# Two stages with rounded operand pairs, four column sums beside stick-breaking, and the first expert rows picked by one-hot products

## What is computed

```python
# first block
mod = silu(c) @ ada_w + ada_b                 # six rows of 1024: shift1, scale1, gate1, shift2, scale2, gate2
y_a = nsa_attention(...) @ w_up_nsa           # 512x512 @ 512x1024
y_b = stick_breaking_attention(...) @ w_up_sb # 512x512 @ 512x1024
mixed = (sigmoid(m_a) * y_a + sigmoid(m_b) * y_b) @ w_out   # 512x1024 @ 1024x1024
h = h + gate1 * mixed
u2 = rms_norm(h, norm2_g) * (1 + scale2) + shift2
h = h + gate2 * (square(relu(u2 @ mlp_w1)) @ mlp_w2)
# second block, its last part: top-1 group of 4, top-2 experts of 8 in it, 32 experts in all
ffn = hierarchical_moe(hn2, ...)   # each expert: (silu(x @ w_gate[e]) * (x @ w_up[e])) @ w_down[e]
x = rms_norm(x + gate2 * ffn, g_final)
```

## Time and profile before

| | |
|---|---|
| median of 3 runs | 1868.61 us (1866.4 to 1873.15) |
| profiled execution, its time | 1867.54 us |
| its span | 1865.8 us |
| PE busy | 1677.0 us, 90% |
| DVE busy | 748.5 us, 40% |
| ACT busy | 482.7 us, 26% |
| POOL busy | 195.3 us, 10% |
| mean granted clock | 0.956 of full |

### The profile page before, as it was taken

The page is one execution under the profiler, slowest core; times in us unless marked ns, Lnnn a source line. Parts: engine busy times, 40 slices in busy tenths (PEclk is TensorE's granted clock), DMA queues, the critical chain, the costliest instruction groups (busy, mean ns, idle before and its releaser), DMA issues. The chain is left out here.

```text
span 1865.8 us, 20533 instructions
## 1 busy us (share of the span) xinstructions
PE 1677.0 (90%) x7854; PEld 1113.4 (60%) x7855; DVE 748.5 (40%) x1298; ACT 482.7 (26%) x799; POOL 195.3 (10%) x260
## 2 busy tenths in 40 slices
PE   5999998988899999999998999889499999998772
PEld 4788887756444778878886778767333333332220
DVE  6344215744565777522225555353411111111113
ACT  4322324545001322222224532252211111110001
POOL 1020000000112122200003000001111111110101
PEclk9999999978999999999999999999699999999996
DMA  9424220020654467522221222105999997999995
GB/s 301 107 68 135 83 76 1 1 91 0 248 183 159 173 238 261 172 77 92 103 98 35 68 91 68 68 1 200 421 402 418 420 380 299 419 418 420 419 420 218
DMA packets 114466, 366.26 MB, mean 196 GB/s; under 512 B 21695, under 2 KB 24939, under 8 KB 89779
## 3 DMA queue, kind: packets, MB, share of 16 engines
q1 hardware_dynamic: 105055, 347.06, 49.4%
q0 software_dynamic: 5760, 9.02, 1.4%
q10 hardware_dynamic: 3540, 8.69, 1.3%
HBM read 359.85 MB, written 16.84 MB: 202 GB/s over the span
## 5 line engine op out<-in xcount | busy, mean ns | idle before, releaser
L2221 PE MATMUL x_upa<-x_ring,x_Ta 128*64 128x512 f32 x608 | 136.8, 599 | 16.4 <-DMA x_ring<-in_w_expert_up_dram 16.4
L2221 PE MATMUL x_gpa<-x_ring,x_Ta 128*64 128x512 f32 x608 | 138.7, 606 | 12.9 <-DMA x_ring<-in_w_expert_gate_dram 10.7
L2221 PEld LDWEIGHTS x_upa<-x_ring,x_Ta 128*64 128x64 f32 x608 | 45.5, 138 | 105.2 <-issue 105.2
L2221 PEld LDWEIGHTS x_gpa<-x_ring,x_Ta 128*64 128x64 f32 x608 | 45.8, 140 | 103.0 <-issue 103.0
L325 DVE TENSOR_TENSOR p_lo<-p_raw,p_hi 128x2048 fp32r<-128x2048 f32 (+1 forms) x20 | 44.8, 2238 | 139.1 <-ACT p_hi L625 139.1
L332 PE MATMUL fr_p<-p_hi,u_high 128*128 128x512 f32 x224 | 89.8, 401 | 0.0
L333 PE MATMUL fr_p<-p_lo,u_high 128*128 128x512 f32 x224 | 88.7, 396 | 0.0
L334 PE MATMUL fr_p<-p_hi,u_low 128*128 128x512 f32 x224 | 88.4, 395 | 0.0
L2246 PE MATMUL x_y0a<-x_ring,x_aTa 128*64 128x512 f32 x304 | 72.9, 600 | 5.6 <-ACT x_aTa L2288 4.5
L2283 ACT ACTIVATE x_siga<-x_gpa 128x512 f32<-128x512 f32 x19 | 11.3, 597 | 253.7 <-PE x_gpa L2221 253.7
L2246 PE MATMUL x_y1a<-x_ring,x_aTa 128*64 128x512 f32 x304 | 71.8, 592 | 0.0
(11 more groups left out here) (770 smaller groups left out, 3822.0 us busy)
## 6 DMA issues: line engine op xcount, KB each, us to landing
x_ring<-in_w_expert_gate_dram SPq DMA_DIRECT2D x64, 1024.0 KB, 23.3
x_ring<-in_w_expert_up_dram SPq DMA_DIRECT2D x64, 1024.0 KB, 27.6
x_ring<-in_w_expert_down_dram SPq DMA_DIRECT2D x64, 1024.0 KB, 25.8
p_raw<-in_w_in_dram SPq DMA_DIRECT2D x18, 1024.0 KB, 5.2
adaw0m<-in_w_ada_dram SPq DMA_DIRECT2D x6, 2048.0 KB, 10.2
adaw1m<-in_w_ada_dram SPq DMA_DIRECT2D x6, 2048.0 KB, 9.5
w_raw0m<-in_mlp_w_dram SPq DMA_DIRECT2D x8, 1024.0 KB, 7.1
w_raw1m<-in_mlp_w_dram SPq DMA_DIRECT2D x8, 1024.0 KB
```

What stands on the lines that cost most here:

```text
L2221: mm = nc.tensor.matmul(ps[CAP * f:CAP * f + CAP, :], self.xT[:, k, CAP * f:CAP * f + CAP], w[m + f][k // 4][:, k % 4, :], start=(k == 0), ...
```

## The change

Four things change.

1. The mixing and the output projection use `matmul3` on rounded pairs. The splitting is done by ACT copies and DVE `low` operations in the same blocks. The separate turning block of the first branch is gone: its flip products stand at the head of `mix_branches`. The turning of the mixture writes high and low parts (`turn_split`).
2. The column sums of modulation units 0 to 3 are made by a new class `FirstSums`, one operation at a time, between DVE's steps of stick-breaking. Unit 4 is summed in the mixing, units 5 to 7 in the output projection.
3. The rows of the first round are no longer gathered. DVE makes a one-hot matrix `picks` (128 places for each tile of tokens), and PE multiplies the normalised rows, which are still in memory, with it: 32 float32 products of 128x128, which come out already turned.
4. The gate products of round 1 move into `norm_route`, ahead of the block's end. The clearing of `x_ga` moves from `norm_route` to the head of `first_places`. In SP's list the load of slot 9, where the normalised rows lie, now comes after the parked slot and also waits for the picking products.

```diff
@@ class FirstSums (new)
+    def load(self, sp):
+        for u, (m, n) in enumerate(self.units):
+            for half in range(2):
+                ks = slice(4 * half, 4 * half + 4)
+                if u:
+                    sp.wait_ge(self.added, KD * (u - 1) + 4 * half + 4)
+                sp.dma_start(self.wbuf[:, ks, :], eights(self.w, m * D + 512 * n, 512)[:, ks, :]).then_inc(self.landed[half], 16)
+    def add(self, dve, count):
+        v = self.nc.vector
+        for j in range(self.done, min(self.done + count, KD * len(self.units))):
+            u, k = j // KD, j % KD
+            a, x, c = self.acc[u], self.wbuf[:, k, :], self.sc[:, k:k + 1]
+            if k % 4 == 0:
+                dve.wait_ge(self.landed[k // 4], 16 * u + 16)
+            if k == 0:
+                v.tensor_scalar(a[:, :], x, c, None, ALU.mult).then_inc(self.added, 1)
+            else:
+                dve.wait_ge(self.added, j)
+                v.scalar_tensor_tensor(out=a[:, :], in0=x, scalar=c, in1=a[:, :], op0=ALU.mult, op1=ALU.add).then_inc(self.added, 1)
@@ stick_breaking, DVE
+                    sums_of.add(dve, 4 if n % 2 else 1 if n else 0)
                     if n >= 3 and n % 2:
                         take((n - 3) // 2)
                     plus(n)
+                    sums_of.add(dve, 1 - n % 2)
                     lows(n)
+                    sums_of.add(dve, 2 * (1 - n % 2))
+                sums_of.add(dve, 1)
                 take(heads // 2 - 1)
@@ mix_branches, PE
+                    if b == 0:
+                        pe.wait_ge(heads_low, 4)
+                        pe.wait_ge(w_low, 1 if n == 0 else 3)
+                    elif n:
+                        pe.wait_ge(w_low, 2)
+                    for k in range(4):
+                        if i == 0 and b == 1:
+                            pe.wait_ge(second_low, 2 * k + 2)
+                        mm = matmul3(nc, ps[i % 2][b][:, :], (high[b][0][:, k, P * t:P * t + P], low_of[b][0][:, k, P * t:P * t + P]),
+                                     (high[b][1 + n][:, k, :], low_of[b][1][:, k, cols(n)]), k == 0, k == 3)
...
+                products(0, 1)
+                products(1, 1)
+                close(0)
+                close(1)
@@ mix_branches, ACT (new)
+                act.wait_ge(w_in[1], 16)
+                for k in range(4):
+                    copy(high[1][1][:, k, :], wu[1][:, k, cols(0)], second_high)
+                    copy(high[1][0][:, k, :], B.oT[1][:, k, :], second_high)
+                for k in range(4):
+                    act.wait_ge(turned, k + 1)
+                    copy(high[0][0][:, k, :], tps[k][:, :], heads_high)
+                act.wait_ge(w_in[0], 16)
+                for b, n in rest:
+                    copy(high[b][1 + n][:, :, :], wu[b][:, :, cols(n)], w_high)
@@ ResidualOut.dve
+        low(v, self.low[0][:, 4:8, :], self.first_w[:, 4:8, :], self.high[1][:, :, 0:512]).then_inc(self.first_low, 1)
+        mod.sum(dve, u)
+        for j in range(2):
+            dve.wait_ge(self.w_high, j + 1)
+            low(v, self.low[1][:, 4 * j:4 * j + 4, :], self.raw[:, 4 * j:4 * j + 4, :],
+                self.high[j][:, :, 512:1024]).then_inc(self.w_low, 1)
+        mod.sum(dve, u + 1)
@@ norm_route, SP
-                sp.wait_ge(stored, 16)
-                ring.load(sp, 9)
                 sp.wait_ge(parked, 16)
                 ring.load(sp, PARKED)
+                sp.wait_ge(stored, 16)
+                sp.wait_ge(first_turned, 4)
+                ring.load(sp, 9)
@@ norm_route, POOL
-                X.begin(pool)
-                pool.wait_ge(X.cleared, 1)
+                X.begin(pool, clear=False)
+                pool.sem_inc(X.ids_ready, 1)
                 pool.wait_ge(stored, 16)
-                pool.wait_ge(tokens, 1)
-                X.gather(pool, 1, 0)
@@ norm_route, PE
+                pe.wait_ge(picked, 1)
+                for k in range(KD):
+                    for t in range(NT):
+                        mm = nc.tensor.matmul(first_ps[k // 2][:, P * (k % 2):P * (k % 2) + P], xn[:, t, cols(k)], picks[:, t, :],
+                                              start=(t == 0), stop=(t == NT - 1))
+                    if k % 2:
+                        mm.then_inc(first_turned, 1)
+                pe.sem_inc(X.turned, 2)
+                table_of(0)
+                w, arrived = ring.of(0), ring.arrived(0)
+                X.half_hidden(pe, 1, w, arrived, 0, 0)
+                table_of(1)
+                X.half_hidden(pe, 1, w, arrived, 0, 1)
@@ residual_up, SP
-                sp.wait_ge(mod1.summed, len(mod1.units))
+                sp.wait_ge(mod1.summed, len(mod1.units) - mod1.first)
                 sp.wait_ge(mod1.spread_out, len(mod1.units))
@@ first_places
+                pool.memset(X.xg[:, :], 0.0).then_inc(X.cleared, 1)
                 X.scatter_nothing(pool)
```

More of the change, by code:

```diff
@@ L141, with __init__ @@
 class Modulation:
-    def __init__(self, s, nc, C, M, cols, w, bias, parts, tag, gain=None):
+    def __init__(self, s, nc, C, M, cols, w, bias, parts, tag, gain=None, summed=0, acc=None):
+        self.first = summed
         self.eights, self.eights_from = {}, []
@@ L1436, in _ @@
             def _(sp):
-                ahead(sp)
+                ahead(sp, sums_of)
             @block.tensor
@@ L1637, in _, with products @@
             def _(sp):
-                for u in range(2, 6):
-                    mod.load_unit(sp, u)
-                    if u == 2:
-                        ahead(sp)
+                load_units(sp)
+                sp.wait_ge(ready, NT)
+                load_first(sp)
+                mod.load_unit(sp, 6)
             @block.tensor
             def _(pe):
-                for i, (t, n) in enumerate(parts):
+                def products(i, b):
+                    t, n = parts[i]
                     if i >= 2:
@@ new lines, in _ @@
+                for k in range(4):
+                    for t in range(NT):
+                        mm = nc.tensor.matmul(tps[k][:, P * t:P * t + P], B.oa[:, t, P * k:P * k + P], C.flip[:, :],
+                                              start=True, stop=True)
+                    mm.then_inc(turned, 1)
+                products(0, 1)
+                products(1, 1)
+                close(0)
+                close(1)
+                for i in range(2, len(parts)):
+                    products(i, 1)
+                    close(i)
@@ L1712, in pe @@
                 for k in range(KD):
[L1713 to L1714 removed]
+                    if b == 0 and k == 4:
+                        pe.wait_ge(self.first_low, 1)
+                    mm = matmul3(self.nc, self.banks[b % 6][:, :], [a[:, k, P * t:P * t + P] for a in self.aT],
+                                 (self.high[k // 4][:, k % 4, 512 * n:512 * n + 512], self.low[n][:, k, :]), k == 0, k == KD - 1)
                 mm.then_inc(self.ready, 1)
@@ L1887, in _, with table_of @@
                 mm.then_inc(counts, 1)
-                for m in range(2):
+                def table_of(m):
                     for h in range(2):
@@ L1917, in _ @@
                 nc.scalar.activation(R.w[:, :, 1:2], d[:, :, :], ACT.Exp).then_inc(exp2, 1)
+                for k in range(4, KD):
+                    act.wait_ge(first_turned, k // 2 + 1)
+                    nc.scalar.activation(X.xT[:, k, :], first_ps[k // 2][:, P * (k % 2):P * (k % 2) + P], ACT.Identity,
+                                         scale=scale[:, k:k + 1], bias=shift[:, k:k + 1]).then_inc(X.modulated[1], 1)
             @block.vector
@@ L2206, in turn, with half_hidden @@
         mm.then_inc(self.turned, 1)
-    def hidden(self, pe, i, w, arrived):
+    def half_hidden(self, pe, i, w, arrived, m, half):
         nc = self.nc
-        for m, ps, ready in ((0, self.gps, self.gate_ready), (2, self.ups, self.up_ready)):
+        ps, ready = (self.ups, self.up_ready) if m else (self.gps, self.gate_ready)
+        if half == 0:
             if m == 0:
@@ L2386, in _, with multiply @@
                 ran = count(pe, "multiply")
-                for b in range(2):
-                    X.turn(pe, 1, b)
-                def multiply(i, w, arrived):
-                    X.hidden(pe, i, w, arrived)
+                def multiply(i, w, arrived, begun=False):
+                    X.hidden(pe, i, w, arrived, begun)
                     X.turn(pe, i + 1, 0)
@@ L3081, in _ @@
                 O.dve(dve)
-                for i in range(NT, NT + 2):
-                    O.take(dve, i)
+                O.take(dve, NT + 1)
                 W.low(dve, 0)
@@ L3340, in program, with load_up @@
                     wu = [beside.sb(f"wu{i}", [P, 4, D]) for i in range(2)]
-                    def load_up(sp):
+                    parts, accs = [2, 4, 3, 5], [M[1].gate[j][:, 512 * n:512 * n + 512] for j in range(2) for n in range(2)]
+                    first_sums = lambda s: FirstSums(s, nc, M[0].sc, A["ada_w"][0], [(m, n) for m in parts[:2] for n in range(2)], accs)
```

(2 more changed lines are left out.)

299 lines of the change are left out of this document (197 added, 102 removed).

## The result

The changed kernel takes 1864.46 us in the median of 20 runs (1854.01 to 1872.3), the kernel before 1871.55 us beside it (1863.28 to 1893.64). The ratio is 0.995, with a 95% interval of 0.9933 to 0.9966: by the ratio 9.4 us less (6.4 to 12.5; the two medians stand 7.1 apart), where 15.7 were forecast. The profiled execution took 1868.54 us, with a span of 1866.7 us at a mean granted clock of 0.950, which is the second slowest of its 20 runs.

The account below looks back on a forecast made before the run. PE was taken to bound mixing, output projection and the experts until about 1550 us, DMA behind that; stick-breaking alternates PE, ACT and DVE. From 1867.5 us, minus 19.8 plus 4.1 gave 1851.8, said as 1852, range 1840 to 1863.

Parts of the forecast that it names:

- Stick-breaking, forecast -2: Stick-breaking: 32 column-sum additions on DVE mostly fit its gaps and lose 2 us, bounds 0 and 25.
- Mixing, +13.8: Mixing, first flip to first turning product: 56.9 us instead of 70.7, with PE standing 1.8; gain 13.8 us.
- Turning, output projection, tail: -0.7, +12.6, -2.9: Split copies lose 0.7 us, cheaper products and one spread fewer gain 12.6, later MLP weights and remainder lose 2.9.
- its 1 us for the clock: Mixing: the granted clock may fall to 0.50 behind PE's new stand; 1 us of loss, bounds 0 and 4.
- The first half as a whole, 19.8: Stick-breaking through output projection and its tail, clock loss included: 19.8 us of gain.
- The join, -4.1: Routing's end to experts' start: picking gains 5.1 us, but the later gather makes PE stand 7.4; net loss 4.1.
- The bound for all of them at the low clock: Routing's end: all 32 picking products at the low clock would give 9 to 10 us of loss.
- DMA doesn't run dry: nothing: Routing's end: slot 9's later load costs nothing, since the parked slot goes ahead and both are queued in time.
- the forecast's reading of the experts: Experts: PE sets the time up to the ring's rest at 1550 to 1570 us, DMA behind it.
- Rival 1: Experts' start: second gather lands before 1362, so picking gains 5.1 us; total 1842.6, chance 0.2.
- Rival 2: First half: half of 11 us of splitting shows, or clock stays low behind stands; gain 10, total 1861.6, chance 0.17.
- Rivals 3 and 4: Mixing's clock falls, slower, up to 1895, chance 0.05; rounded products cost 0.861 us like old ones, 1875, chance 0.03.

Follow-up runs that it names:

- e8: Changed kernel without 28 of the 32 stick-breaking additions, results wrong; single run read only up to the mixing's first flip product, at 470.3 us.
- e2: Kernel before plus only the one-hot picking of first-round rows and the moves that go with it; 1884.2 us, 1.0076 of the kernel before.
- e11: Changed kernel run once more, unaltered, beside e10; 1861.1 us, 0.9945 of the kernel before.
- e1: Changed kernel with picking and its moves taken back, keeping rounded stages and column sums; 1852.67 us, 0.9909 of the kernel before.
- e10: The e1 kernel run once more, beside e11; 1853.92 us, 0.9901 of the kernel before.
- e3: Changed kernel with picking products reading 128 adjacent columns, not every eighth, feature order left wrong; 1855.61 us, 0.9923 of the kernel before.
- e4: Changed kernel with clearings, empty scatter and first scatter addresses moved ahead of the block's edge, so round 2's gather issues earlier; 1855.38 us, 0.9922 of the kernel before.
- e7: The e1 kernel with normalised rows written in the feature order in which products read them; 1855.75 us, 0.990 of the kernel before.
- e5: Changed kernel with normalised rows written in the order products read them, so weights are adjacent columns, nothing left out; 1856.53 us, 0.9926 of the kernel before.
- e6: Changed kernel with e4 and e5, half the first gate products behind the edge, table products side by side; 1859.56 us, 0.9937 of the kernel before.
- e9: e6 with the empty scatter issued at routing's head from a gate's rows, x_outa clearing dropped; 1847.68 us, 0.9873 of the kernel before.
- e12: Changed kernel with SP asking for no weights in the experts' block until round 2's gather lands; single run 1860.84 us, kernel before 1867.59.

## Why the prediction was off

One table of the profiles, in us (e8, whose routing is another, is left out). "Turn" is the first turning product of the mixture, "norm" the first product on `hT`, "rank" the first rank product, "round 2" the turn of round 2, "rest" the time in which DMA's 16 engines rest in the first 300 us behind "rank" (60 windows of 5 us, each at one less its share over 1.015, and never under 0).

| kernel | flip to turn | turn to norm | rank at | rank to round 2 | rank to the span's end | rest |
|---|---|---|---|---|---|---|
| before | 70.7 | 70.2 | 1330.1 | 36.5 | 535.7 | 18.7 |
| e2 join alone | 70.8 | 70.3 | 1336.1 | 46.4 | 545.3 | 28.0 |
| changed | 57.2 | 65.3 | 1319.8 | 46.0 | 546.9 | 28.2 |
| e11 changed | 57.3 | 65.4 | 1312.9 | 46.1 | 546.6 | 28.0 |
| e1 front alone | 57.3 | 62.9 | 1308.5 | 36.5 | 535.7 | 18.7 |
| e10 front alone | 57.4 | 65.6 | 1317.0 | 36.4 | 535.2 | 18.2 |
| e3 adjacent picks | 57.4 | 61.9 | 1313.7 | 40.4 | 540.3 | 22.8 |
| e4 early gather | 57.4 | 65.4 | 1310.9 | 42.0 | 541.1 | 23.4 |
| e7 front, ordered rows | 57.4 | 65.5 | 1318.2 | 36.9 | 535.6 | 20.6 |
| e5 ordered rows | 57.4 | 65.5 | 1309.6 | 39.4 | 538.8 | 23.3 |
| e6 mended | 57.4 | 65.5 | 1315.5 | 40.1 | 538.4 | 23.3 |
| e9 quick edge | 57.4 | 65.4 | 1324.4 | 32.0 | 530.0 | 16.3 |
| e12 quiet gather | 57.2 | 61.9 | 1313.2 | 41.2 | 545.8 | 28.5 |

**Stick-breaking, forecast -2.** In the first profile the flip products came 3.6 us late, but e1 and e4, with the same additions, had them 1 to 2 us early. What differs is the granted clock (0.88 and 0.98 from 402 to 472 us). At a like clock the term is 0 to -0.8: DVE's gaps hold more than the forecast gave them.

**Mixing, +13.8.** It measured 13.3 to 13.6 in all twelve profiles with the front. The step was right: the exposed remainder (1.1 us for 1.8), and the hidden ones. Its instructions stand 0.232 us apart and not 0.227, which takes back what the shorter stand gave.

**Turning, output projection, tail: -0.7, +12.6, -2.9, together +9.0.** Measured 4.7 to 8.3, and under 5 in eight of the twelve. The parts, in us, from the first turning product on (the forecast's turning is 0.7 on top of before):

| | before | forecast | e3 | changed |
|---|---|---|---|---|
| turn to the first output product | 6.1 | 6.8 | 6.5 | 8.5 |
| PE's run of the output projection | 58.7 | 46.1 | 47.5 | 49.1 |
| PE's wait ahead of `norm` | 5.5 | 8.4 | 7.9 | 7.8 |

The run was a little too short in the forecast: 192 instructions at 0.232 instead of 0.227 are 1 us, and the working's own 11.6 and 0.8 make 12.4, not 12.6. The tail was right within 0.6. What was mis-sized most is the clock behind the stands at the two edges of the turning block. The windows of 8 us from the turn on, in the changed kernel and then in e3:

```profile
529.37:537.37 8.00, 6.62 (x32) 6.38 (x32) 5.29 (x8) 4.67 (x8) 0.00 (x0) 0.62 0.00 0
537.37:545.37 8.00, 7.54 (x26) 6.02 (x27) 7.43 (x10) 0.00 (x0) 0.00 (x0) 0.79 0.73 263
```

```profile
527.61:535.61 8.00, 5.90 (x39) 4.65 (x40) 6.38 (x9) 4.45 (x8) 0.00 (x0) 1.00 0.09 12
535.61:543.61 8.00, 8.00 (x36) 6.45 (x35) 6.44 (x9) 0.74 (x1) 0.00 (x0) 1.00 0.68 253
```

The same code gets 0.62 and 0.79 in one execution and 1.00 in another, and takes 3.4 us longer in the first (65.3 and 61.9 from turn to norm). The kernel before had 0.81 and 1.00 in its two windows. The forecast put its 1 us for the clock into the mixing, where none was lost: behind the stand of 1.1 us the products keep their 0.23 us.

**The first half as a whole, 19.8.** By times the front alone gains 17 us (13 to 21) and 18.5 (12 to 25). By the trace, seven profiles with the front and unstrided writes (all but e5, e6, e7 and e9) reach the rank product at 1308.5 to 1319.8, 1313.7 in the mean; the two without it at 1330.1 and 1336.1. The forecast was right within that spread, which is wide for two profiles. Part of it is luck: by the terms above the gain is 17.2 to 21.9, since the additions and the mixing's clock cost less than forecast and the output projection gave less.

**The join, -4.1: this is the step that failed.** In the trace it costs 9.6 to 11.2 us (rank to the span's end), by times 8 (e11 against e10) to 14 (e2). The step, as the prediction put it, was "a 128x128 float32 product takes twice the 0.24 (0.97/4)" at the lower clock and 0.24 at the full one, hence 32 products in 9.1 us. The row was that of the flip products, whose weights are adjacent columns of `qa`. The picking products read every eighth column. They took 0.48 each at the full clock as well, 15.3 in all, and e3 and e5 with adjacent columns took 9.8 and 8.7. So the weights' layout was the price of this term, 5.5 to 6.6 us. The working also has a slip: four us at 0.48 and the rest at 0.24 make 9.7, not 9.1, and e3's adjacent columns took 9.8. The bound for all of them at the low clock, 9 to 10 of loss, was what came, but not through the clock. The rest of the step was right: the stand was 8.2 us for 7.4, the landing 8.9 for 8.5, and the clock behind it was low (from the turn to `x_y1a` 1.8 us more than before, for 1.7).

**"DMA doesn't run dry: nothing" also failed.** DMA's share fell to 0.72 from 1330 to 1350, and over the first 300 us it rests 9.5 us longer, where the forecast had 3. SP's waits between 1300 and 1350 in the changed kernel have the cause:

```profile
SPq L1982 <- PE nr_k L2053: 8.0, 1, 8.0
```

SP stands 8.0 us for the last picking product before it may load slot 9, and issues that load only at 1340.87, when the queue has run dry. Its next load is issued behind the edge, at 1351.22, and in between DMA is idle again. In the table the end follows DMA's rest: the last two columns differ by 514 to 519 in every row. Rest and late PE are not two losses, though. In e12 DMA rests more at first (0.46 from 1330 to 1350), PE's second round begins 4.9 us sooner than in the changed kernel, and the end comes only 1.1 us sooner. The limits change places, as the forecast's reading of the experts said.

**The sum again** with what was measured: 19.4 from the front (1333.1 less 1313.7, the means of two and seven profiles), 9.6 to 11.2 for the join, which leaves 8.2 to 9.8 of gain. The runs have 9.4.

**The rivals.** Rival 1 fell: the join doesn't gain, though e9's trace has a join that does. Rival 2 gives 1861.6, near what came, but not by what it names first: the splitting is hidden, and of its other half, a clock that stays low behind each stand, 3.4 us came in the turning and the output projection, in eight of the twelve profiles. Rivals 3 and 4 fell: the mixing's products keep the full rate, and a rounded product takes 0.70 us, not 0.86.

What stays open is why the clock behind a stand is 0.62 in one execution and 1.00 in the next. The MLP's first product comes anywhere from 592.6 to 601.7 us in profiles of the same front, which is much of the scatter of these times.

## What to carry to other kernels

Take the price of a matmul from a row with the same layout of its weights, not only the same shape: a stride of eight float32 doubled the load of these 128x128 products at the full clock. Look at the drain rows at a block's end: a DMA that POOL had issued shortly before held all engines there until it landed, so issue it early, or first thing behind the edge. When work goes ahead of such an edge to fill PE, list what is issued only behind it (here a gather and the next weights), and what waits for the work itself (here slot 9), since all of it moves back with it.

## What the runs showed of the hardware

- Float32 weights of 128x128: 16 loads in 3.9 us with a stride of eight elements, in 1.9 us adjacent, both at the full clock. At the lower clock the products are nearly level, 19 instructions and 21 in 4.6 us.
- ACT reading a 128x1024 row block with that stride takes 2.1 us where it takes 1.1; two of them 4.17 and 2.19.
- A gather of 128 rows let its reader start 3.5 us behind the issue with DMA nearly idle (one execution) and 8.9 us with the weights' loads under way.
- POOL's drain at a block's end takes 0.04 us with none of its transfers under way, 0.3 us when the last was issued 32 us before, and 7.5 to 8.6 us behind one issued just before.
